# Every third weight piece of the early expert pairs is split by GpSimd instead of VectorE, and reported together with its successor

## The reference

```
qry = xt @ w_query                        # 8 heads, two halves of 128
v1, i1 = top_k(s1, 16);  v2, i2 = top_k(s2, 16)
best, pos = top_k(v1[:, None] + v2[None, :], 16)
gate = softmax(best)
hid = gelu(u_tab[expert] . x)
y = sum over heads and the 16 of  gate * hid * v_tab[expert]
```

## Time and profile before

| what | us |
|---|---|
| median of the runs | 3449.09 |
| profiled execution, its own time | 3446.66 |
| its span, first to last instruction | 3444.9 |
| TensorE busy | 3141.6 (91%) |
| VectorE busy | 2206.3 (64%) |
| ScalarE busy | 1393.4 (40%) |
| GpSimd busy | 29.3 (1%) |

### The profile page before, as it was taken

One profiled execution on the slowest core, in us unless ns is written; L12 is line 12 of the kernel. 1 busy time (PEld: TensorE's weight loads), 2 busy tenths in 40 slices (PEclk: granted clock), 3 DMA queues, 4 the chain that ended last, 5 costly groups with the idle time before them and its releaser, 6 DMA issues. The chain is left out here.

```text
span 3444.9 us, 61131 instructions
## 1 busy us (share of the span) xinstructions
PE 3141.6 (91%) x24050; PEld 2575.3 (75%) x24050; DVE 2206.3 (64%) x3120; ACT 1393.4 (40%) x1699; POOL 29.3 (1%) x32
## 2 busy tenths in 40 slices
PE   7586989999977778999988998999999999999998
PEld 6583878899856667999877977777777777777654
DVE  8765422444366567556547999877777777777654
ACT  3222422454234253346334445444444444444443
POOL 0000000000000002000000000000000000000000
PEclk9878987999899989999999999999999999999999
DMA  5223543555302443334355552466565555566554
GB/s 200 66 75 122 193 152 112 180 195 188 112 1 67 154 139 121 96 123 154 120 192 167 179 163 75 152 195 192 190 195 191 192 191 190 193 196 196 186 194 152
DMA packets 143071, 529.54 MB, mean 154 GB/s; under 512 B 16896, under 2 KB 17664, under 8 KB 140928
## 3 DMA queue, kind: packets, MB, share of 16 engines
q1 hardware_dynamic: 140688, 514.52, 46.0%
q10 hardware_dynamic: 2160, 11.72, 0.9%
HBM read 521.99 MB, written 4.19 MB: 153 GB/s over the span
## 5 line engine op out<-in xcount | busy, mean ns | idle before, releaser
L234 DVE TENSOR_TENSOR mem<-mem,rounded 128x1024 bf16<-128x1024 f32 x952 | 1149.3, 1226 | 733.0 <-ACT rounded L228 725.6
L228 ACT CAST rounded<-mem 128x1024 fp32r<-128x1024 f32 x952 | 988.6, 1047 | 1264.4 <-DMA mem<-weights 390.9
L261 PE MATMUL ps<-rounded 128*128 128x256 f32 x3328 | 467.4, 292 | 53.7 <-DVE mem L234 46.6
L261 PEld LDWEIGHTS ps<-rounded 128*128 128x128 f32 x3328 | 422.2, 194 | 59.5 <-DVE mem L234 30.3
L261 PE MATMUL ps<-mem,rounded 128*128 128x256 bf16 x3328 | 428.9, 276 | 13.3 <-DVE mem L234 13.3
L261 PE MATMUL ps<-rounded,mem 128*128 128x256 bf16 x3328 | 439.2, 279 | 0.0
L261 PEld LDWEIGHTS ps<-mem,rounded 128*128 128x128 bf16 x3328 | 319.5, 99 | 61.1 <-DVE mem L234 9.1
L261 PEld LDWEIGHTS ps<-rounded,mem 128*128 128x128 bf16 x3328 | 316.0, 98 | 62.2 <-issue 1.4
L2344 PE MATMUL ps<-rounded 128*128 128x512 f32 x1024 | 336.1, 442 | 3.0 <-DVE mem L2600 2.1
L2590 DVE TENSOR_TENSOR mem<-mem,ps 128x512 f32<-128x512 f32 x392 | 268.5, 685 | 68.3 <-PE ps L2344 61.2
L2344 PE MATMUL ps<-mem,rounded 128*128 128x512 bf16 x1024 | 307.3, 382 | 0.0
(11 more groups left out here) (405 smaller groups left out, 2441.3 us busy)
## 6 DMA issues: line engine op xcount, KB each, us to landing
mem<-experts SPq DMA_DIRECT2D x512, 512.0 KB, 3.9
mem<-weights SPq DMA_DIRECT2D x440, 512.0 KB, 4.1
mem<-x_t SPq DMA_DIRECT2D x4, 512.0 KB, 10.7
mem<-x_rows SPq DMA_DIRECT2D x1, 2048.0 KB, 8.2
mem<-ln_g ACTq DMA_DIRECT2D x2, 1024.0 KB, 4.9
mem<-ln_b ACTq DMA_DIRECT2D x2, 1024.0 KB, 7.2
mem<-cmp_w_k SPq DMA_DIRECT2D x1, 2048.0 KB, 7.5
mem<-cmp_w_v SPq DMA_DIRECT2D x1, 2048.0 KB, 11.4
```

The costliest lines, as they stand in the source:

```text
L228: self.nc.scalar.copy(self.parts(c % SLOTS)[0], self.raw(c % RAW)).then_inc(self.high_done, 1)
L234: self.nc.vector.tensor_tensor(wl, self.raw(c % RAW), wh.bitcast(F32), ALU.subtract).then_inc(self.low_done, 1)
L261: mm = self.nc.tensor.matmul(self.ps[:, bank, half * 256:half * 256 + 256], a, b, start=(part == 0 and n == 0), stop=(part == PIECES - 1 a ...
```

## The change

`ON_POOL` is `range(E0 + 1, E0 + 63, 3)`: the 21 pieces 441, 444, ..., 501. GpSimd gets a program of its own in the PEER block: for each of them it waits for `high_done` and does the same subtraction, which raises a new semaphore, `pool_low`. VectorE's `low` skips these pieces. At the piece behind each of them (442, 445, ..., 502) it first waits for `pool_low`, then for `high_done`, splits that piece, and raises `low_done` by two. So `low_done` passes over a GpSimd piece only when its successor is split too, for TensorE and for SyncE's loads alike. The remaining pieces (443, 446, ... and 503 on) go as before. The places of `low(n)` in VectorE's order stay where they are.

```
+    pool_low = k.sem("ex_low_on_pool")
+    ON_POOL = range(E0 + 1, E0 + PIECES * LEAD - 1, 3)
...
+        @block.gpsimd
+        def _(pool):
+            for c in ON_POOL:
+                wh, wl = k.parts(c % SLOTS)
+                pool.wait_ge(k.high_done, c + 1)
+                nc.gpsimd.tensor_tensor(wl, k.raw(c % RAW), wh.bitcast(F32), ALU.subtract).then_inc(pool_low, 1)
...
                 for _, c in zip(range(n), early):
-                    k.low(dve, c)
+                    if c - 1 in ON_POOL:
+                        dve.wait_ge(pool_low, ON_POOL.index(c - 1) + 1)
+                        wh, wl = k.parts(c % SLOTS)
+                        dve.wait_ge(k.high_done, c + 1)
+                        tt_(wl, k.raw(c % RAW), wh.bitcast(F32), ALU.subtract).then_inc(k.low_done, 2)
+                    elif c not in ON_POOL:
+                        k.low(dve, c)
```

## The result

The change makes the kernel slower: median 3471.02 us (3466.66 to 3475.47, 4 runs) against 3448.52 us (3443.92 to 3452.28, 4 runs, three of which stood ahead of the prediction), ratio 1.0066 with a 95% interval of 1.0054 to 1.0079. That is +22.5 us, outside the range that was given. The two profiled executions have spans of 3464.9 and 3444.9 us.

A forecast was written before the change was run, and what follows sets the result against it. VectorE was taken to set the pace from about 2010 to 2200 us. +0.6 us before the gates and +3.5 in the gate stage gave +4.1, so 3453 us on the median of 3449.09; range 3443 to 3464.

The forecast's parts named there:

- Bounds: From about 2010 to 2200 us VectorE sets the pace; a microsecond of its time there is one of the kernel's.
- GpSimd's piece: One GpSimd subtraction on 1024 columns takes 2.4 us when VectorE is out of its way.
- The hold: A GpSimd piece holds back a VectorE operation with two SBUF inputs by 1.9 us (1.6 to 2.2).
- a stated sign that the prediction is wrong: In the gate groups, L2565 keeping 0.68 us throughout; about 2.5 us was expected for five of them.
- left as an aside: If L2562 is a two-port tensor-scalar, a lost race in a gate group costs +0.5 us in place of -0.5.
- The gate stage: Pieces 489 to 501: L2565 is 1.8 us late against 1.14 saved, +0.7 us each, +3.5 in all.
- the -5.7 of the sum: Five lows leaving VectorE among the gates save 5 x 1.14 us.
- the tail: From low 481 to the gates, two rounds of raw buffers take 16.4 us instead of 11.6: +4.8 us.
- Stage A: Pieces 441 to 468, to 1997 us: rounds of 8.2 us, VectorE comes to the picks about 2 us earlier.
- stage B: The picks, pieces 469 to 481: -0.1 us in each of two rounds, -1.0 in two more, together -2.2.
- Rival 2: Raw-buffer rounds of 9.1 us decide, mostly before the gates: +12 to +16 us, 3461 us; chance 0.25.
- The offload rival: Search and one-hots don't mind GpSimd, L2565 wins its race among the gates: 3442 to 3446 us; chance 0.13.

The follow-up runs named there:

- The delay kernels: Five low parts left out, no GpSimd, with two or one idle VectorE additions in five gate groups: 3468.12 and 3456.63 us, each against the kernel before's 3450.14.

## Why the prediction was wrong, point by point

**Bounds.** That the loss or gain would be decided by the end of the gate stage held. That "a microsecond of its time there is a microsecond of the kernel's" did not, in one direction. The row for "waits for nobody" was read as if VectorE alone set the pace. Leaving five lows out gave 0 instead of -5.7 us. In a group with a held piece TensorE multiplies that piece and then the product that VectorE's merge waits for, and this takes as long as VectorE's work with the low. I used TensorE's 23 us of spare time in the stage as cover, though it was never spare within one of these groups.

**GpSimd's piece.** 2.4 us were taken; 2.34 at the least and 2.38 in the median were measured. That was right. The estimate of 2.25 us from the Trainium skill (GPSIMD Engine Reference, section Performance versus the Vector engine) was a little low.

**The hold.** 1.9 us taken (1.6 to 2.2), 2.18 measured. The place was another: not L2565 but the one-hot before it, because L2562 itself is held. L2565 kept its length throughout, which was a stated sign that the prediction is wrong:

```profile
L2582 DVE TENSOR_TENSOR mem<-mem x64: 673/684/705, 2059.2 to 2218.5; 128x512 f32<-128x512 f32 x64
```

This is the case that the rule in the Trainium skill (SBUF — State Buffer, section Who interferes with whom) described and that was left as an aside. The trace agrees with it: 2522 ns for one tensor-scalar of 342, and no hold with the source in PSUM.

**The gate stage** is the step that failed: +3.5 forecast, +17.1 measured. 5 x 2.18 = 10.9 us is the hold; nothing comes off it for the five lows (the -5.7 of the sum); the other 6.2, got by subtraction, are what follows on TensorE, which idles 2.3 us, runs at 1.2 GHz after it and makes VectorE wait 12.3 us more. The prediction named no price for an idle TensorE and took its 23 us to spare as cover. The delay kernels show that no property of GpSimd is needed for this part.

**Stages A, B and the tail.** +0.6 forecast, +3.6 to +4.8 measured. The tail was right: 16.4 us from the end of low 481 to the copies (L2547 before), 16.6 measured (2040.2 to 2056.8). The time before the gates moved by 3.9 us (the copies at 2052.95 and 2056.78), over the 3 that were named as a sign of being wrong. Stage A was to bring VectorE to the picks 2 us earlier; they began at 1996.86 and 1997.05. Its rounds up to 1987 took 9.7, 10.0 and 8.4 us and then five times 8.1 to 9.0 (the lows behind a GpSimd piece start at 1916.45, 1926.15, 1936.19, 1944.56, 1953.15, 1961.97, 1970.93, 1979.06, 1987.39), where 8.2 was taken, and one step outside my count was held (the same cast in the kernel before is L2508, shown last):

```profile
1993.15 2.41 POOL L2459 TENSOR_TENSOR mem<-mem,rounded 128x1024 bf16<-128x1024 f32 x1 [5.96 <-ACT rounded L228]
...
1993.31 2.53 DVE L2525 CAST mem<-mem 128x512 f32<-128x512 uint32 x1
...
1995.60 0.43 DVE L2508 CAST mem<-mem 128x512 f32<-128x512 uint32 x1
```

In stage B the first round took 11.6 us instead of 10.3, because the loads behind low 469 landed late (cast at 2005.82, 5.4 us behind the low's end instead of 3.33) and GpSimd then took 3.72 us beside a pick's step. The last two took 9.3 us, as forecast, and the second 9.4, where about 10.3 had been taken.

**The rivals.** Rival 2 was nearest in size (+12 to +16, measured +22.5) but had the wrong place: the ring cost about 4 us, and TensorE showed no wait for a low part before 1999 us, which was its sign. Rounds of up to 9.0 us after 1944 did not starve it there, though the prediction set that limit at 8.4. The offload rival was nearer the truth in the early part than I gave it: the search does not mind GpSimd, and with its own report the early pieces shorten the early part by 3 to 6 us. That the search is not held was assumed and holds (MATCH_REPLACE8 on 128 columns took 0.28 us beside a GpSimd piece, at 1923.21, and has a mean of 276 ns in both kernels).

## What to carry to other kernels

Before work is taken from the engine that seems to bind, leave the work out and time that: here five subtractions on an engine 98% busy were worth nothing, since another engine's work stood in the same place. GpSimd cost nothing here beside the top-16 search and the one-hots from PSUM. A small tensor-scalar from SBUF to SBUF that met it waited for the rest of the GpSimd instruction (2.18 us of 2.35), and the matmuls behind it then ran at a granted clock of 0.50. And a piece should be reported by the engine that made it: in the early part the joint report turned a gain of 4.5 us into a loss of 3.6.

## What was unexpected of the hardware

- A lateness of 2.2 us of the rows' producer cost 3.4 us in the gate stage (17.1 us for five, 18.2 with a delay of VectorE alone), with TensorE's clock at 0.50 after an idle of 2.27 us. One of 1.2 us cost 1.8 (8.9 for five); there the clock fell after one of four idle times of about 1.35 us and not after the other three, and what decides between them is open.
- A one-hot from PSUM is slower than from SBUF, four in 1.36 against 1.11 us, but is not held by GpSimd. A cast from SBUF to SBUF is held (0.43 to 2.53 us).
- Of two loads of 512 KB released together, ScalarE's casts mostly started 1.3 us apart, the first no later than behind a load alone (3.28 us behind low 478, against 3.33). Behind low 469 the first came 2 us late. Why wasn't tried.
